# Expert rows in two phases: gather and dot U, then half of V's columns by dense matrix products and half by gathers

## The reference, cut to what matters

```
def peer(xn, wq, k1, k2, u, v):
    q = (xn @ wq).reshape(B, S, PEER_HEADS, 2, PEER_HALF)
    s1, s2 = ...                       # scores of 128 keys for each half of the query
    t1, i1 = lax.top_k(s1, 16); t2, i2 = lax.top_k(s2, 16)
    cand_s = t1[..., :, None] + t2[..., None, :]
    cand_i = i1[..., :, None] * 128 + i2[..., None, :]
    top_s, pos = lax.top_k(cand_s, 16);  idx = cand_i at pos
    gate = jax.nn.softmax(top_s)
    act = jax.nn.gelu(jnp.einsum('td,ted->te', x_blk, u[i_blk]))      # E = 8 * 16 picks
    return jnp.einsum('te,ted->td', gate * act, v[i_blk])
```

## Time and profile before

| what | value |
|---|---|
| time, median of 2 runs | 3284.99 us (3284.85 to 3285.13) |
| the profiled execution: span | 3284.6 us, 0.4 us under the median of the runs |
| TensorE busy | 2819.1 us (86%) |
| VectorE busy | 1834.5 us (56%) |
| ScalarE busy | 1188.8 us (36%) |
| GpSimd busy | 666.9 us (20%) |
| DMA, mean over the span | 375 GB/s, 1230.51 MB |
| DMA, in the expert stages | 430 to 431 GB/s |

### The profile page before, as it was taken

How to read it: one execution, slowest core, us unless ns; L and a number is a source line. 1 busy time by engine, 2 the same in 40 slices (tenths; PEclk the granted TensorE clock), 3 DMA queues, 4 the chain that set the end, 5 groups by cost and what they waited for, 6 DMA issues and landing times.

```text
span 3284.6 us, 25042 instructions
## 1 busy us (share of the span) xinstructions
PE 2819.1 (86%) x8456; PEld 1530.1 (47%) x8456; DVE 1834.5 (56%) x2733; ACT 1188.8 (36%) x3551; POOL 666.9 (20%) x573
## 2 busy tenths in 40 slices
PE   7999999889987877777879999988898787777777
PEld 6887765444442323323338786544444233333332
DVE  4454555555555555555656755555555555555554
ACT  4344433333333333333343542333333333333333
POOL 1000022222222222222210002222223222222221
PEclk9999999999999999999999999999999999999999
DMA  6554599999999999999995349999999999999998
GB/s 227 183 187 141 202 383 430 430 430 431 431 430 431 431 431 431 431 431 431 431 406 168 128 147 381 430 430 431 430 431 431 431 431 431 431 431 431 430 431 373
DMA packets 139198, 1230.51 MB, mean 375 GB/s; under 512 B 12984, under 2 KB 13760, under 8 KB 68160
## 3 DMA queue, kind: packets, MB, share of 16 engines
q0 software_dynamic: 74016, 1073.77, 76.4%
q1 hardware_dynamic: 61680, 147.99, 12.7%
q10 hardware_dynamic: 3376, 7.18, 0.6%
HBM read 1226.79 MB, written 2.11 MB: 374 GB/s over the span
## 4 chain that ended last, share of the span: by engine, by line
PE 45%; DMA 41%; DVE 7%; ACT 4%; issue 2%; POOL 0%; ACTq 0%; SPq 0%; DVEq 0%; POOLq 0%
DMA ring_sb<-in_peer_uv_dram,idx_cur 39%; PE bank L1250 20%; PE bank L985 15%; PE bank L1032 6%; DVE ring_sb L1772 5%; PE bank L1044 1%; ACT diag L810 1%; ACT shared L801 1%; ACT shared L799 1%; DMA ring_sb<-in_peer_uv_dram,idx_half 1%; PE bank L1195 1%; DVE w_parts L402 1%; DMA ring_sb<-in_mlstm_w_out_dram 0%; ACT w_parts L396 0%; ACT shared L793 0%
## 5 line engine op out<-in xcount | busy, mean ns | idle before, releaser
L1250 PE MATMUL bank<-ring_sb,diag 128*128 128x512 f32 x4080 | 1906.1, 615 | 424.2 <-ACT diag L810 421.8
L1772 DVE CUSTOM_DVE_ANT_0 ring_sb<-ring_sb,arena 128x2048 f32<-128x2048 f32 x512 | 1173.3, 2292 | 1110.0 <-DMA ring_sb<-in_peer_uv_dram,idx_cur 1072.7
L1250 PEld LDWEIGHTS bank<-ring_sb,diag 128*128 128x128 f32 x4080 | 764.2, 194 | 1519.7 <-issue 807.9
L582 POOL DMA_INDIRECT ring_sb<-in_peer_uv_dram,idx_cur x494 | 590.2, 1195 | 1834.7 <-PE bank L1250 1828.0
L793 ACT ACTIVATE shared<-shared 128x1 f32<-128x1 f32 x512 | 103.7, 203 | 1576.5 <-DVE shared L1772 1576.4
L985 PE MATMUL bank<-w_parts,actT_hi 128*128 128x512 f32 x1664 | 520.5, 394 | 8.0 <-DVE w_parts L402 6.3
L402 DVE TENSOR_TENSOR w_parts<-ring_sb,w_parts 128x2048 fp32r<-128x2048 f32 x100 | 229.4, 2299 | 211.5 <-ACT w_parts L396 211.3
L985 PEld LDWEIGHTS bank<-w_parts,actT_hi 128*128 128x128 f32 x1664 | 310.0, 189 | 74.7 <-issue 9.6
L396 ACT CAST w_parts<-ring_sb 128x2048 fp32r<-128x2048 f32 x100 | 190.6, 1909 | 272.2 <-DMA ring_sb<-in_mlstm_w_in_dram 134.3
L985 PE MATMUL bank<-w_parts,actT_lo 128*128 128x512 f32 x640 | 250.3, 391 | 0.0
L810 ACT ACTIVATE diag<-const,shared 128x128 f32<-128x128 f32 x510 | 204.9, 402 | 16.6
(11 more groups left out here) (190 smaller groups left out, 1134.2 us busy)
## 6 DMA issues: line engine op xcount, KB each, us to landing
ring_sb<-in_mlstm_w_in_dram SPq DMA_DIRECT2D x48, 1024.0 KB, 5.1
ring_sb<-in_attn_w_in_dram SPq DMA_DIRECT2D x20, 1024.0 KB, 5.0
ring_sb<-in_mlstm_w_out_dram SPq DMA_DIRECT2D x16, 1024.0 KB, 4.9
arena<-in_peer_wq_dram SPq DMA_DIRECT2D x16, 1024.0 KB, 18.5
ring_sb<-in_attn_w_out_dram SPq DMA_DIRECT2D x16, 1024.0 KB, 4.9
wq_more<-in_peer_wq_dram SPq DMA_DIRECT2D x12, 1024.0 KB, 16.4
ring_sb<-in_peer_uv_dram,idx_cur POOLq DMA_INDIRECT x494, 21.0
ring_sb<-in_peer_wq_dram SPq DMA_DIRECT2D x4, 1024.0 KB, 8.4
```

The costliest lines, as they stand in the source:

```text
L582: nc.gpsimd.indirect_dma_start(out=uv_slot[at], out_offset=None, in_=uv_rows, in_offset=bass.IndirectOffsetOnAxis(ap=rows_at[:, k:k + 1], ...
L1250: last = mm(acc[n][:, :], diag[slot_of(gu, k)][:, :], v_slot[at][:, n * CH:(n + 1) * CH], start=False, stop=end, skip_group_check=True)
L1772: v.tensor_tensor_reduce(u_slot[at], u_slot[at], xn[b], 1.0, 0.0, ALU.mult, ALU.add, dots[:, k:k + 1]).then_inc(dot_done, 1)
```

## The change: what it does

The table is split into `u` (16,384 rows of 8 KB), the right half of `v`'s columns (`vg`, rows of 4 KB, gathered) and the left half (`vd`, stored so that 128 experts with the same `i1` lie together, 4 KB rows). A layer now runs in two phases.

Phase 1: the ring holds twelve slots of 1 MB. Only `u` rows are gathered and dotted. The weights gelu times gate are kept in `w_all` (128 picks for each token), the pick numbers in `pair_all` and `idx_all`. There is no diagonal matrix and no product with `v`.

Weight matrices: for each block the numbers `i1`, `i2` and the weights are transposed (`picks_transposed`). For each token a 128 x 128 product of a one-hot matrix (pick by `i2`) with a weighted one-hot matrix (pick by `i1`) gives that token's weights for all 16,384 experts. Four tokens make a group, 32 groups make a block: ScalarE and VectorE build the operands (`onehot_group`, `weighted_group`), TensorE multiplies (`weights_group`), ScalarE copies the result to SBUF. Block 0's groups are placed one after every second dot from the third dot of unit 8 on. Block 1's run after the last dot.

Phase 2: `dense` reads all of `vd`, 64 loads of 1 MB over SyncE into three slots, and multiplies: 128 groups of experts x 2 blocks x 2 pieces of 512 columns, 512 products in a layer. Meanwhile the 256 tiles of `vg` (0.5 MB each) are gathered into six slots and VectorE adds each, weighted, to the residual (`add_value`). At the end VectorE adds the four PSUM banks.

In layer 0 the weights of chunk 16 are loaded during phase 2 and split there, but the normalisation of both blocks, the transposes and the split of block 0 now come after the last addition.

```diff
-        NUV = NDIAG = 6
-        RING = 2 * NUV
+        RING = 12
+        NU = 12
+        ND, NG = 3, 6
+        DENSE = 1024
 # SyncE
+            def load_dense(l):
+                for p in range(D_PAIRS):
+                    if p < ND:
+                        sp.wait_ge(dot_done, l * LAYER_TILES + LAYER_TILES - 8 + p + 1)
+                    else:
+                        sp.wait_ge(vd_used, l * D_PAIRS + p - ND + 1)
+                    sp.dma_start(d_slot[p % ND].rearrange("p (i n) -> p i n", n=DENSE),
+                                 vd_tab[l][2 * p:2 * p + 2].rearrange("i p n -> p i n")).then_inc(vd_landed[p % ND], 16)
+                    if l == 0 and p in KEYS_BEHIND:      # p = 28, 36, 44, 52: a quarter of chunk 16
...
 # GpSimd, gathers(l)
-                            nc.gpsimd.tensor_copy(idx_cur[par][:, :], idx_next[:, :]).then_inc(idx_taken, 1)
-                        pool.wait_ge(v_used, gu * TOPK + (k + 1))
-                            out=uv_slot[at], out_offset=None, in_=uv_rows,
+                        if i >= NU:
+                            pool.wait_ge(dot_done, l * LAYER_TILES + i - NU + 1)
+                            out=ring[i % NU], out_offset=None, in_=u_tab[l],
+            def values(l, j):
+                b, p = G_ORDER[j]
+                if j < 2:
+                    pool.wait_ge(idx_ready, (l + 1) * UNITS)
+                elif j < 4:
+                    pool.wait_ge(dot_done, l * LAYER_TILES + LAYER_TILES - NU + 8)
+                elif j < NG:
+                    pool.wait_ge(dot_done, (l + 1) * LAYER_TILES)
+                else:
+                    pool.wait_ge(vg_added, l * NB * PICKS + j - NG + 1)
+                nc.gpsimd.indirect_dma_start(out=g_slot[j % NG], out_offset=None, in_=vg_tab[l], ...)
 # ScalarE
-                        nc.scalar.activation(diag[slot_of(gu, k)][:, :], ident, ACT.Copy,
-                                             scale=e_w[:, c]).then_inc(diag_ready, 1)
+                def onehot_group(b, g):
+                    if done >= 2:
+                        act.wait_ge(wb_full, done - 1)
+                    for j in range(GROUP):
+                        st.did(nc.scalar.activation(onehot_2[g % 2][:, j, :], numbers, ACT.Abs,
+                                                    bias=picks_T[:, P + t:P + t + 1], scale=-1.0))
+                    st.need(st.n)
+                    nc.scalar.activation(onehot_2[g % 2], onehot_2[g % 2], ACT.Relu, bias=1.0,
+                                         scale=-1.0).then_inc(onehot_act, 1)
+                def weights_group(b, g):
+                    act.wait_ge(wb_full, (2 * l + b) * GROUPS + g + 1)
+                    copy(dst, mis[g % 2][:, :].rearrange("p (t i) -> p t i", i=P)).then_inc(wb_out, 1)
+                picks_copied(1)
+                onehot_group(1, 1)
+                for g in range(GROUPS):
+                    weights_group(1, g)
+                    if g % 2 and g + 2 < GROUPS:
+                        onehot_group(1, g + 2)
 # TensorE
-                        for n in range(4):
-                            last = mm(acc[n][:, :], diag[slot_of(gu, k)][:, :], v_slot[at][:, n * CH:(n + 1) * CH], ...)
+                def weights_group(b, g):
+                    pe.wait_ge(weighted_ready, done + 1)
+                    if done >= 2:
+                        pe.wait_ge(wb_out, done - 1)
+                    for j in range(GROUP):
+                        last = mm(mis[g % 2][:, j * P:(j + 1) * P], onehot_2[g % 2][:, j, :], weighted_1[g % 2][:, j, :], ...)
+                def dense():
+                    pe.wait_ge(wb_out, (2 * l + 2) * GROUPS)
+                    for p in range(D_PAIRS):
+                        pe.wait_ge(vd_landed[p % ND], 16 * uses(p, l, ND, D_PAIRS))
+                        for i in range(2):
+                            for b in range(NB):
+                                for n in range(2):
+                                    last = mm(acc[2 * b + n][:, :], experts_W[b][:, e * P:(e + 1) * P],
+                                              d_slot[p % ND][:, i * DENSE + n * CH:i * DENSE + (n + 1) * CH], ...)
+                        last.then_inc(vd_used, 1)
 # VectorE
+                def weighted_group(b, g):
+                    if at >= 2:
+                        dve.wait_ge(wb_full, at - 1)
+                    for j in range(GROUP):
+                        last = v.tensor_scalar(weighted_1[g % 2][:, j, :], numbers, picks_T[:, t:t + 1],
+                                               picks_T[:, 2 * P + t:2 * P + t + 1], ALU.is_equal, ALU.mult)
+                    if b == 1 and g % 2 == 0:
+                        v.tensor_tensor(onehot_2[0], ..., ALU.is_equal).then_inc(onehot_dve, 1)
+                def add_value():
+                    dve.wait_ge(vg_landed[j % NG], 16 * uses(j, l, NG, NB * PICKS))
+                    v.scalar_tensor_tensor(out=xb[b][:, DENSE:D], in0=g_slot[j % NG], scalar=w_all[b][:, p:p + 1],
+                                           in1=xb[b][:, DENSE:D], op0=ALU.mult, op1=ALU.add).then_inc(vg_added, 1)
                 for u in range(UNITS):
                     unit(u)
-                last_tile()
+                for g in range(GROUPS):
+                    weighted_group(1, g)
+                    if g % 4 == 3:
+                        add_value()
+                while added[0] < NB * PICKS:
+                    if l == 0 and added[0] in KEYS_SPLIT:
+                        lo_weights(dve, 16, [KEYS_SPLIT.index(added[0])])
+                    add_value()
+                ...        # then four additions of acc to xb[b][:, 0:DENSE]
 # VectorE after peer(0)
-            lo_weights(dve, 16, [1])
+            norm_ms(2, 0)
             norm_ms(2, 1)
+            norm_rows(2, 0, 3)
+            lo_groups(dve, "n2", range(2))
```

More of the change, by code:

```diff
@@ L147, in trunk_kernel @@
         iota = const[:, C_IOTA:C_IOTA + 16]
+        numbers = const[:, C_IOTA:C_IOTA + P]
         gelu_c = const[:, C_GELU:C_GELU + 1]
@@ L571, in gathers @@
                             norm(2 * l + 1, [1])
+                        if i == 2 * FIRST_QUERY_SLOT:
                             pool.wait_ge(rq_full, l * (HEADS + 1) + 2)
[L573 to L581 removed]
@@ L587, in _, with experts @@
+            def experts(l):
+                gathers(l)
+                for j in range(NB * PICKS):
+                    values(l, j)
             first_rows()
@@ L593, in _ @@
             norm(1, [0])
-            gathers(0)
-            norm(2, [1])
+            experts(0)
+            norm(2)
             for n in range(5):
@@ L599, in _ @@
             norm(3, [0])
-            gathers(1)
+            experts(1)
         @block.scalar
@@ new lines, in dense @@
+                def dense():
[3 more added lines that the diff above has]
+                        for i in range(2):
+                            e = 2 * p + i
+                            for b in range(NB):
+                                for n in range(2):
+                                    last = mm(acc[2 * b + n][:, :], experts_W[b][:, e * P:(e + 1) * P],
+                                              d_slot[p % ND][:, i * DENSE + n * CH:i * DENSE + (n + 1) * CH],
+                                              start=(e == 0), stop=(e == P - 1), skip_group_check=True)
+                                    if e == P - 1 and (b, n) != (1, 1):
+                                        last.then_inc(bank_done, 1)
+                        last.then_inc(vd_used, 1)
@@ L1266, in peer @@
                     unit(u)
-                pe.wait_ge(x_out, 4 * (NB * l + 1))
-                seed(1)
-                for u in range(HEADS, UNITS):
-                    unit(u)
+                picks_transposed(0)
+                pe.wait_ge(sc_out, (l + 1) * (HEADS + 1))
+                for g in range(GROUPS):
+                    weights_group(0, g)
+                picks_transposed(1)
+                for g in range(GROUPS):
+                    weights_group(1, g)
+                dense()
             peer(0)
```

385 lines of the change are left out of this document (205 added, 180 removed).

## The result

The changed kernel takes **3355.8 us** (median of 2 runs, 3354.53 to 3357.06) against 3284.99: ratio 1.021, 95% interval 1.018 to 1.024. The forecast was 3305 us and no change that can be told. The time lies inside the range, but the change is a slowdown clear of the noise (whether it is more than 2% is open, as the interval holds 1.02), and 50 us are missing from the sum.

The account below looks back on a forecast made before the run. VectorE bounds phase 1, hand-overs the step between, DMA phase 2: 1287 us in layer 0 against 1280.8, 1277 against 1277.0. So 3284.6 + 0 + 6 + 9 + 5 gives 3305 us, range 3250 to 3410.

Parts of the forecast that it names:

- Phase 1: Gathers and dots of `u` rows: 735 us a layer, 725 to 760, bound by VectorE.
- near 360: Sign to look for in phase 1: a DMA rate near 360 GB/s.
- with each term at its better end: Lower end of the range for the whole kernel: a sum of 3250 us.
- GpSimd falls behind: Rival between two dots: waiting gather issue not let in or delaying the next dot, 205 us a layer, 3715; chance 0.05.
- Phase 2's length: Dense products and `vg` gathers: DMA at 412 GB/s, 473 us in layer 0, 463 in layer 1; 4 for last additions.
- The rival of slow 4 KB rows: Phase 2 loads at 346 GB/s: 552 us, 89 more a layer, 3483 in all; chance 0.10.
- that of a slow TensorE clock: Rival in phase 2: TensorE bounds it, taking 880 us at 1.2 GHz, 4125 in all; chance 0.02.
- Between the phases: From last dot through block 1's 32 groups: 75 us a layer, 62 to 90, decided by hand-overs.
- The rival of groups one behind the other: Between the phases, each group waits for three engines in turn: 150 us, 75 more a layer, 3455; chance 0.09.
- The step to attention: From layer 0's last addition into attention: normalisation no longer covered, 9 us more, 6 to 14.

Follow-up runs that it names:

- experiment 1: Changed kernel with each dot taking 1024 of its 2048 columns, gathers and their bytes whole: 3220.5 us.
- experiment 4: Changed kernel with each addition taking 64 of its 1024 columns, every load whole: 3327.6 us.
- experiment 5: Changed kernel with each addition of a V tile waiting for the one before it to be finished: 3348.8 us.
- experiment 3: Changed kernel without 61 of the 64 dense loads in each layer: 3251.8 us; then with additions of 64 columns too: 3250.5 us.

## Why the prediction was right and where it failed

**Phase 1: right.** Bound by VectorE (experiment 1), 735 against 738.6 and 740.4, dots 2.21 us apart. The excess of 3.6 and 5.4 us stands beside waits of dots for landings, 11.0 us in layer 0, all of them before 700 us, where the rate is 420 GB/s at share 1.01. There the DMA engines are full: the query weights that I left out of the bytes of phase 1 are loaded there. The rate of "near 360" holds only for the later part. Two slips in the working did no harm: 44.4 less 35.5 us is 8.9 for a choice of experts, not 8.4, and the 3250 "with each term at its better end" leaves out the better rate of 421 GB/s, with which it would be about 3230.

**GpSimd falls behind: wrong for the dots, right for the additions.** Between two dots the waiting issue got in every time and VectorE was not delayed: 396 issues in phase 1 ended 0.80 to 0.86 us after the dot in which they began, and the next dot started 2.22 us after the one before, against 2.21 where no issue waited. Timelines of both in phase 1 of the changed kernel:

```profile
905.06 2.29 DVE L1888 CUSTOM_DVE_ANT_0 ring_sb<-ring_sb,actT_sb 128x2048 f32<-128x2048 f32 x1
907.27 0.09 DVE L1888 DVE_READ_ACCUMULATOR2_ANT shared<- 128x1 f32 x1
907.27 2.30 DVE L1888 CUSTOM_DVE_ANT_0 ring_sb<-ring_sb,actT_sb 128x2048 f32<-128x2048 f32 x1
...
905.23 2.93 POOL L600 DMA_INDIRECT ring_sb<-in_peer_u_dram,idx_all  x1 [0.31 <-issue]
908.47 1.92 POOL L600 DMA_INDIRECT ring_sb<-in_peer_u_dram,idx_all  x1 [0.30 <-issue]
```

But phase 2's sentence, "GpSimd's gather at 0.94 us, or up to 0.8 past an addition, also fits", is **the step that failed**. It compared each engine by itself with the 1.9 us of the mixed stretch, not with the 1.28 us that a gather has once the dense loads are through, and so the sum had nothing for the end of phase 2. And it took one addition as the longest hold; it is the whole row of additions without a gap. The runs showed 26 us for the additions at the two ends (experiment 4), of which the hold is about 7 (experiment 5). The Trainium skill (SBUF — State Buffer, Who interferes with whom and Summary: rules for kernel authors) says that a DVE instruction with two SBUF inputs contends with a GpSimd instruction that reads SBUF, and that who comes second is blocked fully; the trace agrees, with 6.52 us for an issue of 0.94, and adds that the block can outlast several instructions.

**Phase 2's length: the bound of its middle right, its ends mis-sized.** The bytes decide in the middle (experiments 3 and 4), at 407 to 409 GB/s, not 412: about 5 us a layer. I spread this rate over the whole stage and gave its start 2.5 us; its two ends cost 12.4 and 13.7 us a layer (experiment 4). I had the last gather landing 10 to 30 us behind the last product. The addition of the last tile began 51 and 43 us behind it, as 34 and 30 tiles were still to add when it was done. Together these are 36 of the 41 us. The last 5 are all in layer 0. There phase 2 moved 198.0 MB (394 GB/s over it) against 192.7 in layer 1 (395 GB/s), 5.3 MB more where the sum had 4.2; that is about 3 us at 408 (an estimate), and the rest stays open. The rival of slow 4 KB rows is refuted by the 408 of experiment 3, and that of a slow TensorE clock by the 1.00 granted in the middle of phase 2. The Trainium skill (SBUF — State Buffer, Summary: rules for kernel authors) counts with about 358 GB/s; here gathers alone ran at 408.

**Between the phases: right, by compensating errors.** 73.1 and 74.3 against 75. The copy from PSUM took more than its price. It writes with a stride, which is the difference that the two kernels' code shows; no run tried it by itself. The groups by shape in the changed kernel:

```profile
L848 ACT COPY ring_sb<-bank 128x512 f32<-128x512 f32 x64 | 66.6, 1041 | 22.1 <-PE bank L1306 22.1
```

The row taken was a contiguous copy of the same size at 0.57 us. Two groups still took 4.0 us, and 4.9 with an addition among them, on the mean the 4.4 that I took; what made up for the copy was not measured. The rival of groups one behind the other did not occur. **The step to attention** cost 10.9 us against 9.

**Where 67 MB a layer went.** Layer 1 as stretches, from first dot to last addition: the kernel before, then phase 1, the step and phase 2 of the changed one.

```profile
2004.33:3281.34 1277.01, 1062.29 (x2603) 481.77 (x2601) 712.48 (x1077) 439.76 (x1593) 315.20 (x269) 0.98 1.00 428
```

```profile
2049.26:2789.68 740.42, 211.45 (x805) 175.49 (x803) 721.85 (x1181) 418.84 (x1522) 476.50 (x256) 0.58 0.95 378
2789.68:2863.96 74.28, 48.29 (x259) 42.71 (x259) 57.02 (x157) 60.83 (x118) 11.09 (x10) 0.75 0.24 78
2863.96:3351.75 487.79, 441.40 (x1024) 195.12 (x1024) 316.20 (x250) 0.00 (x0) 301.31 (x243) 0.95 1.00 395
```

At 431 GB/s the bytes of the last three (280, 6 and 193 MB) would take 90, 61 and 41 us less than they did, 192 us in all, where the kernel before lost 10. That outweighs the 156 us that the saved bytes are worth (an estimate from these rates). Before, 4.87 us of DMA time a tile ran under everything. Now VectorE's phase 1 leaves the DMA engines idle about a tenth of the time for most of it, the step between the phases leaves them three quarters idle for 74 us, and the rate of 4 KB rows is 408 in place of 431. The forecast had most of this and came to 0.6% slower; the ends of phase 2 are the largest part of what took it to 2.1%. I had given 0.28 to a slowdown beyond 2%, nearly all of it on single large rivals and 0.02 on a sum of small excesses; it was the sum of small excesses.

## What to carry to other kernels

When a loop that overlaps everything is cut into phases, price the ends of each phase by the engines that are left there, not by the rate of its middle, and put work of the next phase into the idle transfer time of the step between: dropping one `if` was worth 48 us here. Where GpSimd must issue gathers, try a gap between two-input VectorE instructions: it freed the held gather here and was worth some 7 us. An idle ScalarE can take element work from a VectorE that bounds a phase even at 2.8 times the time (3.2 against 1.12 us a group); that brought the kernel from 0.5% over to 0.5% under the time before.

## What the hardware showed beyond that

- A waiting gather issue is let in between two dots, although they follow each other at 2.21 us, but at the start of phase 2 not between additions 1.20 us apart; at 1.39 us apart it is. In phase 1 of the changed kernel 20 issues that began within 0.02 us of a dot's start were not held at all (0.94 us), and their dots took 2.34 us instead of 2.29; the 396 that began 0.15 us or more into a dot were held. But in the gather-only end of the changed kernel, additions 1.27 us apart ((5.10 - 1.28) / 3) let short issues through; what decides was not isolated. Its timelines of VectorE and GpSimd:

```profile
3305.89 5.10 DVE L1879 SCALAR_TENSOR_TENSOR x_sb<-actT_sb,gate_rows,x_sb 128x1024 f32<-128x1024 f32 x4
...
3307.01 0.97 POOL L615 DMA_INDIRECT ring_sb<-in_peer_vg_dram,idx_all  x1 [0.30 <-issue]
3308.29 0.98 POOL L615 DMA_INDIRECT actT_sb<-in_peer_vg_dram,idx_all  x1 [0.30 <-issue]
```

- 4 KB rows, gathered alone or mixed with in-order loads, 407 to 409 GB/s; 8 KB rows 421; 16 KB rows 431.
- A ScalarE copy of 128 x 512 from PSUM: 0.57 us contiguous, 1.04 us where neighbouring elements land 512 bytes apart.
